# Forming decay matrices and beta scalings during a convolution and storing them, and two more slots for expert weights

## The reference

```python
qkv = silu(short_conv(qkv, conv_w))             # 3 taps along the tokens
g = cumsum(log_a)                               # per head, inside a chunk
gam = exp(where(tri, g[..., :, None] - g[..., None, :], -inf))
m = where(strict, einsum('nbhid,nbhjd->nbhij', kb, kc) * gam, 0)     # kb = k * beta
# (m + 1) is inverted, and a recurrence over chunks carries a state s
a_qk = einsum('nbhid,nbhjd->nbhij', qc, kc) * gam
```

```python
xs = h[idx]                                     # 64 latents (32 context tokens) per expert
hid = silu(xs @ w_gate[e]) * (xs @ w_up[e])
y = hid @ w_down[e] * gate                      # added back to the chosen tokens
```

## Time and profile before

| | us |
|---|---|
| median of three executions | 2351.53 (2346.67 to 2352.14) |
| the profiled execution, its time | 2348.14 |
| its span, first to last instruction | 2346.3 |
| TensorE busy | 2112.7 (90%) |
| VectorE, ScalarE, GpSimd busy | 754.1, 447.9, 121.2 |
| moved by DMA | 551.32 MB, mean 235 GB/s |
| mean granted TensorE clock | 0.943 of full |

### The profile page before, as it was taken

How to read it: one execution, slowest core, us unless ns; L and a number is a source line. 1 busy time by engine, 2 the same in 40 slices (tenths; PEclk the granted TensorE clock), 3 DMA queues, 4 the chain that set the end, 5 groups by cost and what they waited for, 6 DMA issues and landing times.

```text
span 2346.3 us, 33291 instructions
## 1 busy us (share of the span) xinstructions
PE 2112.7 (90%) x13898; PEld 1075.5 (46%) x13898; DVE 754.1 (32%) x1436; ACT 447.9 (19%) x1018; POOL 121.2 (5%) x119
## 2 busy tenths in 40 slices
PE   5998999818689969999999998999999599999997
PEld 3544656518686423333333334554674244444442
DVE  2143523588775331101001113000772412221113
ACT  2223421485311110000000012000561000000001
POOL 0000000030111000001111000000000000000000
PEclk9999999957678979999999999999999799999999
DMA  7219730123125259999999982110313499999996
GB/s 290 72 50 365 252 126 19 38 72 109 55 80 188 103 217 369 397 395 396 400 385 400 403 346 89 54 45 0 113 42 153 174 401 421 421 421 421 421 421 274
DMA packets 110619, 551.32 MB, mean 235 GB/s; under 512 B 13024, under 2 KB 25824, under 8 KB 61328
## 3 DMA queue, kind: packets, MB, share of 16 engines
q1 hardware_dynamic: 102512, 522.29, 56.4%
q0 software_dynamic: 7168, 23.83, 3.5%
q10 hardware_dynamic: 800, 3.15, 0.3%
HBM read 525.27 MB, written 22.38 MB: 233 GB/s over the span
## 4 chain that ended last, share of the span: by engine, by line
PE 75%; DMA 11%; DVE 8%; ACT 3%; issue 2%; SPq 1%; POOL 0%; DVEq 0%; POOLq 0%; ACTq 0%
PE ps L2296 22%; PE ps L2308 5%; PE ps L508 5%; DMA work_sb<-expert_w_up 4%; PE ps L1798 4%; PE ps L911 4%; DMA ring_sb<-expert_w_up 3%; PE ps L2666 3%; PE ps L1839 2%; PE ps L2638 2%; PE ps L2647 2%; PE ps L2326 2%; DMA ring_sb<-ada_w 2%; PE ps L2346 2%; PE ps L910 2%
## 5 line engine op out<-in xcount | busy, mean ns | idle before, releaser
L2296 PE MATMUL ps<-work_sb 128*32 128x512 f32 (+1 forms) x2432 | 409.7, 595 | 11.4 <-ACT work_sb L2428 5.5
L2296 PE MATMUL ps<-ring_sb,work_sb 128*32 128x512 f32 (+1 forms) x2048 | 299.9, 599 | 13.1 <-DMA ring_sb<-expert_w_up 8.6
L2296 PEld LDWEIGHTS ps<-work_sb 128*32 128x32 f32 (+1 forms) x2432 | 123.3, 120 | 234.6 <-issue 227.3
L2296 PEld LDWEIGHTS ps<-ring_sb,work_sb 128*32 128x32 f32 (+1 forms) x2048 | 87.3, 118 | 201.3 <-issue 194.7
L2487 DVE TENSOR_TENSOR work_sb<-ps,work_sb 128x512 f32<-128x512 f32 x32 | 20.6, 686 | 437.3 <-PE ps L2308 329.1
L2418 ACT ACTIVATE work_sb<-ps 128x1024 f32<-128x1024 f32 x16 | 16.4, 1024 | 513.9 <-PE ps L2308 294.2
L508 PE MATMUL ps<-ring_sb,work_sb 128*128 128x512 f32 (+1 forms) x288 | 108.1, 537 | 0.9 <-DVE work_sb L403 0.9
L2308 PE MATMUL ps<-ring_sb,work_sb 128*32 128x512 f32 x768 | 101.1, 597 | 0.0
L2308 PE MATMUL ps<-work_sb 128*32 128x512 f32 x768 | 100.6, 592 | 0.0
L911 PE MATMUL ps<-work_sb,ring_sb 128*128 128x512 f32 x192 | 98.1, 592 | 0.0
L2506 DVE SCALAR_TENSOR_TENSOR work_sb<-ps,work_sb,gates_sb 128x1024 f32<-128x1024 f32 x16 | 20.5, 1284 | 232.8 <-PE ps L2308 124.8
(11 more groups left out here) (426 smaller groups left out, 2910.4 us busy)
## 6 DMA issues: line engine op xcount, KB each, us to landing
work_sb<-expert_w_down SPq DMA_DIRECT2D x88, 1024.0 KB, 18.6
work_sb<-expert_w_gate SPq DMA_DIRECT2D x64, 1024.0 KB, 7.1
ring_sb<-expert_w_gate SPq DMA_DIRECT2D x64, 1024.0 KB, 10.8
ring_sb<-expert_w_up SPq DMA_DIRECT2D x64, 1024.0 KB, 15.0
work_sb<-expert_w_up SPq DMA_DIRECT2D x56, 1024.0 KB, 14.3
ring_sb<-ada_w SPq DMA_DIRECT2D x96, 512.0 KB, 5.6
ring_sb<-expert_w_down SPq DMA_DIRECT2D x32, 1024.0 KB, 13.5
ring_sb<-wout SPq DMA_DIRECT2D x16, 512.0 KB, 5.9
```

The source lines that it names most:

```text
L2296: mm = pe.matmul(ps[g:g + wide, bank + n, :], lat_src[:, k, g:g + wide], us[e][:, n * 512:(n + 1) * 512], start=(k == 0), stop=(k == KT - 1))
```

## The change

1. The 12 blocks are formed during the convolution. SP loads the spread rows in three batches (n 0 to 4, 5 to 8, 9 to 11; five buffers, three of them in free halves of H). ScalarE does the Abs of a batch after its part of given tiles (`ABS_AT`) and the Exp (`EXP_AT`). GpSimd makes two products from each: the beta-scaled block in a single buffer `BETA`, the masked block in place. SP stores both, to `beta_rows` and `mask_rows`, and loads the next batch when the stores of the last are done. `dn_sync` later loads them into RM(g) and EB(n).
2. ScalarE's Abs, Exp and beta work, GpSimd's beta products and VectorE's mask products leave the preparation.
3. Layer 1 has 14 expert slots instead of 12. Slots 4 to 10, 12 and 13 are filled first, 0 to 3 as soon as the ring is free, 11 after the stores. The last normalised tile is stored from ScalarE's queue. SP's loop of layer 1 is unrolled. Slot 13 has its two rows apart, so all expert transfers are written with two pieces of one row each.

```diff
+        PREP = [(tt, d) for pair in GROUPS for tt in pair for d in range(2)]
+        DECAYS = [range(0, 5), range(5, 9), range(9, 12)]
+        ABS_AT = {0: (0, 1), 1: (2, 3, 4), 4: (5, 6), 5: (7, 8), 7: (9,), 8: (10, 11)}
+        EXP_AT = {1: DECAYS[0], 5: DECAYS[1], 8: DECAYS[2]}
+        DECAY_AT = [0, 1, 2, 3, 4, 0, 1, 3, 4, 0, 1, 2]
+        BETA = region(19288, 1024, "p (t h n) -> p t h n", t=2, h=4)
...
@@ conv_act, in tile c, after its copies and Silu
+                for n in ABS_AT.get(c, ()):
+                    decay_act(act, n)
+                for n in EXP_AT.get(c, ()):
+                    decay_exp_act(act, n)
                 if c == CONV_TILES - 2:
+                    act.wait_ge(tile_out[3], 16 * (DECAYS[1][-1] + 1))
                     dnorm_act(act)
...
+        def decay_act(act, n):
+            tt, d = PREP[n]
+            if n in [batch[0] for batch in DECAYS]:
+                act.wait_ge(dc_in, 32 * decays_to(n))
+            for h in range(8):
+                e = DECAY(n)[:, h // 4, h % 4, :]
+                last = nc.scalar.activation(e, e, ACT.Abs, bias=GB[:, tt, d, 0, h:h + 1], scale=-1.0)
+            last.then_inc(dn_e, 1)
+
+        def decay_exp_act(act, n):
+            act.wait_ge(dn_e, first_decay(n) + n + 1)
+            nc.scalar.activation(DECAY(n), DECAY(n), ACT.Exp, scale=-1.0).then_inc(dn_e, 1)
...
+        def decay_pool(pool, n):
             tt, d = PREP[n]
+            pool.wait_ge(dn_e, decays_to(n) + n + 1)
+            if n >= 1:
+                pool.wait_ge(tile_out[0], 16 * n)
+            beta = GB[:, tt, d, 1, :].rearrange("p (t h) -> p t h", t=2)
+            nc.gpsimd.tensor_tensor(BETA, DECAY(n), bc(beta.unsqueeze(3), [P, 2, 4, P]), ALU.mult).then_inc(dn_rb, 1)
+            mask = AMASK[:, d, :].unsqueeze(1).unsqueeze(1)
+            nc.gpsimd.tensor_tensor(DECAY(n), DECAY(n), bc(mask, [P, 2, 4, P]), ALU.mult).then_inc(dn_rb, 1)
...
+        def decays_in(sp, batch):
+            for n in batch:
+                tt, d = PREP[n]
+                for half in range(2):
+                    first = 16 * d + 4 * half
+                    sp.dma_start(DECAY(n)[:, half], gb_rows[first:first + 4, tt * P:(tt + 1) * P].partition_broadcast(P))                         .then_inc(dc_in, 16)
+
+        def decays_first(sp):
+            sp.wait_ge(gq_pv, PAIRS)
+            sp.wait_ge(gq_o, NT)
+            sp.dma_start(AMASK, t["masks"].rearrange("p (d n) -> p d n", d=2)).then_inc(masks_in, 16)
+            sp.wait_ge(g_rows, 16)
+            decays_in(sp, DECAYS[0])
+
+        def decays_sync(sp):
+            for b, batch in enumerate(DECAYS):
+                for n in batch:
+                    sp.wait_ge(dn_rb, 2 * n + 1)
+                    sp.dma_start(beta_rows[n].rearrange("p (t h n) -> p t h n", t=2, h=4), BETA).then_inc(tile_out[0], 16)
+                    sp.wait_ge(dn_rb, 2 * n + 2)
+                    sp.dma_start(mask_rows[n].rearrange("p (t h n) -> p t h n", t=2, h=4), DECAY(n)).then_inc(tile_out[3], 16)
+                if b + 1 < len(DECAYS):
+                    sp.wait_ge(tile_out[3], 16 * (batch[-1] + 1))
+                    decays_in(sp, DECAYS[b + 1])
...
@@ prep_dve: betas come loaded, the masks are in the loaded EB
+                if s == 0:
+                    dve.wait_ge(rm_in[g % 2], 64 * (g // 2 + 1))
...
-                step.mark(nc.vector.tensor_tensor(EB(n), EB(n), bc(AMASK[:, d, :].unsqueeze(1), [P, 8, P]), ALU.mult))
...
@@ dn_sync
+            sp.wait_ge(w_free, U_CONV + CONV_TILES)
+            sp.wait_ge(tile_out[0], 16 * 2 * NT)
+            sp.wait_ge(tile_out[3], 16 * 2 * NT)
+            betas(0)
             for n in range(4):
                 decay(n)
+            betas(1)
             spill_group(0)
             spill_group(1)
+            sp.wait_ge(dn_lp, lp(G64_, 0, 1, 1))
+            betas(2)
...
@@ stream_units: decays_first comes behind the weights of convolution tile 7; decays_sync behind those of tile 11
@@ experts
-        SLOTS = (8, 12)
+        SLOTS = (8, 14)
...
+                    first_rows(sp, l, [*range(4, SLOTS[0])] if l == 0 else [*range(4, 11), 12, 13])
...
+            sp.wait_ge(w_free, U_MOE[l])
+            first_rows(sp, l, range(4))
+            if l == 1:
+                sp.wait_ge(mp["stored"], 16 * (2 * NT + LT))
+                first_rows(sp, l, (11,))
...
-            sp.dma_start(to.rearrange("p j n -> p (j n)"), src).then_inc(land, 16)
+            sp.dma_start(to, src).then_inc(land, 16)
```

More of the change, by code:

```diff
@@ L1021, in build @@
         dn_qk, dn_zero = sem("dn_qk"), sem("dn_zero")
-        dn_grow, dn_spill = ([sem(f"dn_{n}{b}") for b in range(4)] for n in ("grow", "spill"))
-        dn_back = [sem(f"dn_back{b}") for b in range(2)]
+        row_land, tile_out = ([sem(f"{n}{b}") for b in range(4)] for n in ("row_land", "tile_out"))
+        tile_in = [sem(f"tile_in{b}") for b in range(2)]
         (dn_e, dn_rb, dn_t, dn_kt, dn_qt, dn_rm, dn_eye, dn_v, dn_wd, dn_lp, dn_la, dn_ld, dn_cp, dn_cd, dn_ktl, dn_ok, dn_ra) = (
@@ L1027, in build, with spilled @@
         GT_, V32_, G64_, VAB_ = range(4)
+        def spilled(b, count):
+            return 16 * (count + (2 * NT if b in (0, 3) else 0))
         def lp(stage, g, t_, d=1):
@@ L1287, in dn_pe @@
             chunks_pe(pe, *RUNS[2])
[L1289 to L1305, removed]
         def pack_act(act, g):
             for s in range(4):
-                act.wait_ge(dn_rm, 8 * g + s + 1)
+                act.wait_ge(dn_rm, muls(g, s) - 4)
                 for b in range(4):
@@ L1627, in dn_pool @@
         def dn_pool(pool):
+            pool.wait_ge(masks_in, 32)
+            for n in range(2 * NT):
+                decay_pool(pool, n)
             pool.wait_ge(cv_c, CONV_TILES)
             nc.gpsimd.memset(S.rearrange("p d q n -> p (d q n)"), 0.0)
-            for n in range(4):
-                beta_pool(pool, n)
             pool.wait_ge(cv_tr, CONV_TILES)
+            pool.wait_ge(tile_out[3], 16 * 2 * NT)
             eye_pool(pool, 0)
@@ L2078, in build @@
         LATE = [region(first, 2 * D, "p (j n) -> p j n", j=2) for first in (15360, 17408)] + [
-            H[:, 0:2, :], region(0, 2 * D, "p (j n) -> p j n", j=2)]
-        late_land = [sem(f"late_land{s}") for s in range(4)]
-        SLOTS = (8, 12)
+            H[:, 0:2, :], region(0, 2 * D, "p (j n) -> p j n", j=2), GATE[:, 1]]
+        apart = region(27648, D)
+        LATE.append(bass.AP(apart.tensor, apart.offset, [apart.ap[0], [31137 - 27648, 2], [1, D]]))
+        late_land = row_land + tile_in
+        SLOTS = (8, 14)
         TOPS = region(29640, 2 * CAP_L)
@@ L2268, in landings @@
             n = 24 * p + i
-            first = u0 // RING + 3 * NPAIR * l if i % SLOTS[l] < 8 else 0
+            s = n % SLOTS[l]
+            first = u0 // RING + 3 * NPAIR * l if s < 8 else 3 if s < 12 else 6
             return first + n // SLOTS[l] + 1
@@ L2288, in product @@
                         i = 8 * m + k // 2 * 2 + e
-                        rows, land = place(l, i)
+                        rows, land = place(l, 24 * p + i)
                         pe.wait_ge(land, 16 * landings(l, p, i, u0))
@@ L2936, in stream_units @@
                     sp.dma_start(slot, t["wconv"][args[0]]).then_inc(sig, 16)
+                    if args[0] == 7:
+                        decays_first(sp)
                 elif kind in ("wout0", "wout1", "wv"):
```

119 lines of the change are left out of this document (54 added, 65 removed).

## The result

The kernel after took 2363.91 us (median of ten executions; nine lie from 2356.45 to 2365.82, one took 12090.64 and is left out of the ratio), the kernel before 2348.85 beside it: ratio 1.0046, 95% interval 1.0033 to 1.0060. (The ratio is given as recorded; the quotient of these two medians would be 1.0064.) In a later comparison it was 1.0039 (1.0027 to 1.0052). The forecast was 2343.7, and its range ended at 2357. The profiled execution took 2364.67 (span 2362.9).

What follows compares the result with a forecast made beforehand. The prediction took the chain as 75% TensorE, with DMA the bound in layer 1's experts. Convolution lateness 18.4, savings 21.2 behind it and 5.0 in the experts gave -7.8 us: 2343.7 against the median 2351.53, range 2332 to 2357.

Steps and rivals of the forecast that it cites:

- Savings behind the convolution: Preparation and recurrence: ready-made blocks save 12.0 us in group 0, 4.6 each in groups 1 and 2; -21.2 us in all.
- Experts: Layer 1's experts: DMA-bound, 178 transfers remain instead of 180 with 14 slots, -5.0 us; layer 0 unchanged.
- The moved loads: Layer 1's experts: earlier first loads go out where DMA is mostly idle and cost 0.
- Rival 5: Experts: rows go out in 4 KB pieces, costing +21 us, net +13, 2357 us; chance 0.05.
- the lateness of the convolution: Convolution: the last tile ends 18.4 us later because ScalarE waits for loads and TensorE behind it; bounds 14 to 25.
- stand while batch 1 is late: Convolution: ScalarE waits in tile 4 for the second batch's loads until 397.5; TensorE stands 8.5 us.
- the tile behind it: Convolution, after each stand: ScalarE's queued Abs, Exp, table loads, copies and Silu delay TensorE another 2.7, then 1.7 us.
- stand while batch 2 is late: Convolution: ScalarE waits from 420.5 for the third batch's loads, landed at 441; TensorE stands 5.5 us.
- The string: Convolution: beta product, store, landing and next product follow one another on one buffer, 4.9 us a step.
- Cost taken 0, bound 0 to 5: Convolution: GpSimd products meeting VectorE's two-input operations were taken to cost 0, bound 0 to 5 us.
- The clock: Convolution: a lower TensorE clock after the 8.5 us stand may cost 1.7 us, swallowed by a 2.7 us wait; counted 0.
- Rival 2: Convolution: stores land as in a queue; 2350 us at a 3.6 us landing, 2363 at 5.0; chance 0.15.

Runs made afterwards that it cites:

- after again: The kernel after, unchanged, measured a second time against the kernel before: ratio 1.0039.
- ScalarE later: The kernel after with ScalarE's second-batch work at tiles 7 and 8 instead of 4 and 5, the third's behind tile 11: ratio 1.0007 to before.
- The run without the last batch's products: The kernel after with a second beta buffer and no GpSimd products for the last three blocks, stored as ScalarE left them: ratio 0.9971 to before.
- two beta buffers: The kernel after with a second buffer for beta products, so GpSimd forms one while the other is stored: ratio 0.9979 to before.
- groups 0 and 1: The kernel after with eight blocks in the convolution, second batch's ScalarE work at tiles 6 and 7: ratio to before 0.9906 with two beta buffers, 0.9907 with one.
- the decays alone: The kernel after without its expert part, the twelve blocks still formed in the convolution: ratio 1.0045 to before.

## Why the prediction was wrong

**What held.** The mechanism and its two places: ScalarE waits at tiles 4 and 7 for batches 1 and 2, TensorE behind it. Savings behind the convolution 19.9 us (10.6, 4.9, 4.4) for 21.2. Experts 4.3 for 5.0, though not every time: of eleven profiles with 14 slots nine took 479.3 to 479.7 us from layer 1's first expert matmul to the end (483.9 before), but after again 482.5 and ScalarE later 482.7, with a clock granted at 0.90 and 0.89 in their first 60 us and 0.95 in after's. The moved loads hid. Rival 5 is out: layer 1's experts move 420 GB/s (421 before), and only the slot whose rows lie apart sends short packets. Of a 360 us stretch, before first and then after:

```profile
DMA packets 20793, 151.59 MB, mean 421 GB/s; under 512 B 2304, under 2 KB 2304, under 8 KB 2304
```

```profile
DMA packets 22032, 151.27 MB, mean 420 GB/s; under 512 B 2302, under 2 KB 2302, under 8 KB 4862
```

The 2560 more under 8 KB are the two 4 KB pieces of one slot in fourteen (144 transfers / 14 x 128 x 2 = 2633).

**The step that failed** is the lateness of the convolution: 18.4 forecast, 33.0 measured, outside my bounds of 14 to 25. In its own terms:

| term | forecast | measured |
|---|---|---|
| stand while batch 1 is late | 8.5 | 13.7 |
| the tile behind it | 2.7 | 3.0 |
| stand while batch 2 is late | 5.5 | 8.1 |
| the tile behind it | 1.7 | 1.5 |
| last tile: sums, squares, transposes | 0 | 6.7 |

(Measured against the 10.98 us of a tile.)

- *The string.* I took 2.8 us for a landing, 1.9 for a product and 0.2 for hops, 4.9 a step. The first landing took 5.13 (issued right behind the weights of tile 11), the second 4.34, the third and fourth 2.62; the first batch's four steps took 24.2 us for 19.6, its loads were issued at 392.4. The first loads took 9.8 from issue to landing for my 9.4, the next 8.4 for 7.4.
- *GpSimd and VectorE.* "Cost taken 0, bound 0 to 5" was wrong twice. Beside VectorE's taps a product takes 2.2 to 3.07 us instead of 1.89 and 2.35 (the mask product, which I had put at 1.90 like the beta product, is 2.35 alone), and in program order it keeps the next beta product waiting: that is the 2.67 of GpSimd's L1610 in the chain at 376.75. And the taps become 2.5 to 3.0 us for 1.02, which delays VectorE's sums of squares, ScalarE's squares behind them, and the last transposes by 5 to 7 us. I had looked for whom the product delays and not for whom the tap delays. The run without the last batch's products shows 5.1 of it. This agrees with the rule of the Trainium skill that I weighed (SBUF — State Buffer, "SBUF: two separate sides"): a two-input VectorE operation and a GpSimd one do not overlap on SBUF; its size on a term depends on who waits.
- *The clock.* After the stand TensorE's clock was granted at 0.50, the lower of 1.2 and 2.4 GHz, until about 415: six transposes take 1.51 us for 0.82, and tile 7 takes 13.98 for 10.98. I had 1.7 for it, swallowed by ScalarE's 2.7; it is TensorE's own 3.0, and no engine is waited for. That 2.7 and 1.7 come so near to 3.0 and 1.5 is luck: they were put down to another wait.

Rival 2 had the place and the direction (a mean landing of 3.6 us: it was 3.7 in the first batch, 3.1 in the second) and gave 2350 there; with the 6.7 us of the last tile this is 2357. Its 2363 was for landings of 5.0 us, which were not there: it lies next to the 2364 measured by luck. Rival 5's price was added up wrongly: a net of +13 is 2365 on the median before of 2351.5, as the other rivals are counted, not 2357, and so outside the stated range; the packets above rule it out whatever its price.

**What is left** is 4.5 us between group 2 and the out projection, and 3.0 in layer 0. The first goes with the granted clock: over this stretch it is 0.72 before (117.4 us), 0.70 in both profiles of after (121.9 and 122.1), 0.73 with two beta buffers (117.1), and TensorE is busy for 102.0 us in both of after and for 97.4 before, with 1284 or 1285 matmuls recorded in each. In both the full clock comes back later. The 10 us that begin 30 us behind group 2's transpose, before first and then after:

```profile
640.50:650.50 10.00, 8.74 (x78) 8.60 (x78) 8.03 (x18) 0.00 (x0) 0.61 (x1) 1.00 0.15 54
```

```profile
653.10:663.10 10.00, 10.00 (x59) 10.00 (x58) 5.64 (x11) 0.00 (x0) 0.80 (x1) 0.62 0.00 0
```

The seven profiles with all twelve blocks in the convolution run from 116.9 to 122.1 on the same code. Why the clock comes back later in some, and whether the change has a part in it, is open. The second is scatter: this stretch took 569.4 to 579.5 us over all thirteen profiles, 572.5 and 579.5 in the two of groups 0 and 1. With 13.0 us at group 2's transpose and 4.3 back in the experts, 8.7 us are explained, 0.37% of the 0.46%, inside the interval.

## What to carry to other kernels

Work moved under a busy engine has to meet that engine's order, not its idle share: ScalarE was idle for 9 us a tile here, and one load that came 27 us after its place in ScalarE's program cost TensorE 13.6 us. When a later piece of such work depends on a round trip of the piece before, take only as many pieces as come round in time; here eight of twelve, with the experts, gave 22 us, and the last four took 20 of them back. Put the first user of a load where it has landed even at its longest; with eight blocks a second buffer was then worth nothing.

## What the runs showed of the hardware

- A VectorE operation of 1.02 us with two SBUF inputs takes 2.5 to 3.0 us beside GpSimd's products, and even the one-input tap 2.04 for 0.62; GpSimd's take 2.2 to 3.07 for 1.9 and 2.35.
- Lone 0.5 MB stores landed in 2.6 us for the most part, but the beta store of a batch's second block took 4.3 to 4.6 us in after and 3.2 to 4.7 with the decays alone. In the second batch this store took 4.63 in after and 2.61 in ScalarE later, issued 2.4 us behind the mask store before it in either; what tells the two apart was not found.
- A full-speed TensorE that stood 13.6 us ran at 0.50 until some 6 us after it resumed, and the tile cost 3.0 us more; after a stand of 8.0 us 1.5 more.
